# Where the operands of a matmul stand in SBUF: shifts of 32, 64 and 256 bytes

## The reference

```python
def _swiglu(x, w_gate, w_up, w_down):
    return (jax.nn.silu(x @ w_gate) * (x @ w_up)) @ w_down
...
h = _layer_norm(ALPHA * h + 0.5 * _swiglu(h, ffn1...), ln1_g, ln1_b)
mix = _token_mixers(h, w_in, ...)                  # 1024 -> 3072, recurrence and gating, -> 1024
h = _layer_norm(ALPHA * h + mix, ln2_g, ln2_b)
xa = _memory_cross_attention(h, mem, ...)          # q, k, v and output, 1024 x 1024 each
h = _layer_norm(ALPHA * h + xa, ln3_g, ln3_b)
h = _layer_norm(ALPHA * h + 0.5 * _swiglu(h, ffn2...), ln4_g, ln4_b)
...                                                # second block
h = rmsnorm(x, norm1_g)
x = x + concatenate([attention_mixer(...), pool_mixer(...)]) @ w_out
h = rmsnorm(x, norm2_g)
x = x + (silu(h @ w_gate) * (h @ w_up)) @ w_down
```

## Time and profile before

| | |
|---|---|
| median of the two runs | 1665.95 us |
| profiled execution, span | 1663.7 us |
| TensorE busy, matmuls | 1653.9 us (99%), 8375 |
| weight loads, beside the matmuls | 1393.3 us (84%) |
| GpSimd, VectorE, ScalarE busy | 704.5, 629.7, 597.6 us |
| mean granted TensorE clock | 0.999 of full |
| transfers | 157.58 MB, mean 95 GB/s |

### The profile page before, as it was taken

One profiled execution on the slowest core, in us unless ns is written; L12 is line 12 of the kernel. 1 busy time (PEld: TensorE's weight loads), 2 busy tenths in 40 slices (PEclk: granted clock), 3 DMA queues, 4 the chain that ended last, 5 costly groups with the idle time before them and its releaser, 6 DMA issues.

```text
span 1663.7 us, 20763 instructions
## 1 busy us (share of the span) xinstructions
PE 1653.9 (99%) x8375; PEld 1393.3 (84%) x8375; DVE 629.7 (38%) x1059; ACT 597.6 (36%) x911; POOL 704.5 (42%) x392
## 2 busy tenths in 40 slices
PE   9999999999999999999999999999999999999999
PEld 7888888899888888889888888898768988888888
DVE  4111121257565777656121111257763512121122
ACT  4122222247545555436221222247574322122220
POOL 4454444554572443133454444444323444344442
PEclk9999999999999999999999999999999999999999
DMA  7333243333222444123333243351113333323332
GB/s 208 91 102 92 83 117 89 101 104 111 77 64 64 127 129 144 57 77 89 91 99 101 74 117 99 92 156 42 44 32 80 86 101 93 97 83 110 99 89 77
DMA packets 296041, 157.58 MB, mean 95 GB/s; under 512 B 5265, under 2 KB 292618, under 8 KB 295946
## 3 DMA queue, kind: packets, MB, share of 16 engines
q1 hardware_dynamic: 295946, 156.26, 32.8%
HBM read 154.14 MB, written 2.10 MB: 94 GB/s over the span
## 4 chain that ended last, share of the span: by engine, by line
PE 93%; DVE 3%; ACT 2%; issue 1%; DMA 1%; POOL 0%; SPq 0%; DVEq 0%; POOLq 0%
PE bank L551 22%; PE bank L552 22%; PE bank L555 22%; PE bank L2349 2%; PE bank L2353 2%; PE bank L2350 2%; PE bank L594 2%; PE bank L595 2%; PE bank L599 2%; PE bank L2846 2%; PE bank L574 1%; PE bank L580 1%; PE bank L575 1%; PE bank L2834 1%; PE bank L2375 1%; PE bank L2594 1%
## 5 line engine op out<-in xcount | busy, mean ns | idle before, releaser
L479 POOL TENSOR_TENSOR wlo<-wraw,whi 128x1024 fp32r<-128x1024 f32 (+1 forms) x238 | 561.4, 2372 | 771.3 <-ACT whi L474 771.3
L551 PE MATMUL bank<-ahi,whi 128*128 128x512 f32 x1294 | 507.8, 392 | 0.0
L552 PE MATMUL bank<-alo,whi 128*128 128x512 f32 x1294 | 503.8, 389 | 0.0
L474 ACT CAST whi<-wraw 128x1024 fp32r<-128x1024 f32 (+1 forms) x268 | 268.0, 1025 | 232.6 <-PE bank L555 152.9
L555 PE MATMUL bank<-ahi,wlo 128*128 128x512 f32 x1294 | 320.9, 389 | 0.0
L551 PEld LDWEIGHTS bank<-ahi,whi 128*128 128x128 f32 x1294 | 243.0, 188 | 51.4 <-issue 1.2
L552 PEld LDWEIGHTS bank<-alo,whi 128*128 128x128 f32 x1294 | 242.9, 188 | 51.2 <-issue 1.4
L555 PEld LDWEIGHTS bank<-ahi,wlo 128*128 128x128 f32 x1294 | 242.9, 188 | 50.4
L1649 DVE SCALAR_TENSOR_TENSOR hval<-gate,bank 128x512 f32<-128x512 f32 x66 | 45.4, 687 | 554.4 <-PE bank L555 540.2
L1044 ACT ACTIVATE gate<-bank 128x512 f32<-128x512 f32 x66 | 39.5, 598 | 512.8 <-PE bank L555 500.6
L1658 DVE SCALAR_TENSOR_TENSOR res<-res,bank 128x512 f32<-128x512 f32 x78 | 52.7, 685 | 236.3 <-PE bank L555 163.8
(11 more groups left out here) (380 smaller groups left out, 2285.0 us busy)
## 6 DMA issues: line engine op xcount, KB each, us to landing
wraw<-in_ffn_w_gate SPq DMA_DIRECT2D x42, 512.0 KB, 3.9
wraw<-in_ffn_w_up SPq DMA_DIRECT2D x42, 512.0 KB, 3.9
wraw<-in_ffn_w_down SPq DMA_DIRECT2D x32, 512.0 KB, 3.6
wraw<-in_w_in SPq DMA_DIRECT2D x30, 512.0 KB, 4.0
wraw<-in_w_gate SPq DMA_DIRECT2D x21, 512.0 KB, 3.9
wraw<-in_w_up SPq DMA_DIRECT2D x21, 512.0 KB, 3.9
wraw<-in_w_out SPq DMA_DIRECT2D x16, 512.0 KB, 5.2
wraw<-in_w_down SPq DMA_DIRECT2D x16, 512.0 KB, 3.7
```

The costliest lines, as they stand in the source:

```text
L474: eng.copy(high_of(b)[:, 0:n], raw_of(b)[:, 0:n]).then_inc(hi_ready, 1)
L479: eng.tensor_tensor(low_of(b)[:, 0:n], raw_of(b)[:, 0:n], high_of(b)[:, 0:n], ALU.subtract).then_inc(LO[b][0], 1)
L551: eng.matmul(o, w, xhi[:, k, :], start=(k == 0), stop=False)
L552: eng.matmul(o, w, xlo[:, k, :], start=False, stop=False)
```

## The change

Two things change. First, the places of three tiles. `ahi` starts 32 bytes further, `alo` 64 bytes further than they would without a gap, and the tiles behind them move up by 512, so that their remainders stay; `hid` starts 256 bytes lower. The remainders modulo 512 are then: `ahi` 160, `alo` 192, `wraw`, `wlo`, `whi` 128 as before, `hid` 384, the early tiles 192 as before. Second, `multiply_tokens` finds its slots by the places in the rings and not by the block's own number. For the high weights that is the same slot (284 and 268 are both 0 modulo 4). For the low weights it is another: 284 modulo 6 is 2, 276 modulo 6 is 0, and the two blocks' low parts lie in slots 0 and 1.

The instructions and their order are the same on every engine.

```diff
@@ -111,8 +111,10 @@
         res = sb("res", [P, KD, T])
-        ahi = sb("ahi", [P, KD, T], F32R)
-        alo = sb("alo", [P, KD, T], F32R)
+        base = top[0]
+        ahi = sb("ahi", [P, KD, T], F32R, at=base + 32)
+        alo = sb("alo", [P, KD, T], F32R, at=base + 64 + KD * T * 4)
+        top[0] = base + 2 * KD * T * 4 + ROW
         wbase = top[0]
         wraw = sb("wraw", [P, RAW, SLOT])
@@ -151,7 +153,7 @@
         WORK = 16 * KB
-        take = region(WORK)
+        take = region(WORK - ROW // 2)
         hid = take("hid", [P, max(PARTS), 2, T], F32R)
@@ -2488,7 +2490,7 @@
             def multiply_tokens(ph):
                 b = ph.base + LAST
-                at = b % 4, b % RAW
+                at = HI_AT[b] % 4, RAW_AT[b] % RAW
                 wait_hi(pe, b + 1)
```

## The result

The changed kernel takes 1684.09 us at the median (1683.87 to 1684.31) against 1665.95 before: ratio 1.0113, 95% interval 1.0094 to 1.0132. It is 18.1 us slower, clear of noise and under 2%. The forecast was 1667, so the time is inside the range, but by the branch in which full blocks lose their settled pace (which I gave 0.13 for a loss under 2%), and not by the one I took. That the range holds it is owed to its width and not to the mechanism I chose.

What follows compares the result with a forecast made beforehand. The prediction took TensorE's matmul pace, busy 99% of the span, as the bound. Span 1663.7 plus 1.2 us (halved blocks; all other terms 0) gave 1664.9, plus 2.25 from span to median 1667.1, forecast 1667, range 1622 to 1699.

Steps and rivals of the forecast that it cites:

- the full blocks lose the settled pace: Rival: 512-column matmuls off distance 0 slow by 4.5 ns (+24.5 us) or to 232 ns (+29 us); chance 0.22, 0.13 under 2%.
- What bounds it: Whole kernel: TensorE busy 99% of 1663.7 us, almost no idle time to win, so only its matmul pace is left.
- Step 1: Full blocks, 5448 matmuls of 512 columns: pace stays 226.7 ns, change 0; bounds -66 to +29 us.
- the rival of a gain: Distance frees the full blocks: 17, 36 or 66 us less (1650, 1630, 1600); chances 0.10, 0.13, 0.11, together 0.34.
- My upper bound of 5.3 ns a matmul: Full blocks: up by the worst pace seen at this width, 232 ns; +5.3 x 5448 = +29 us.
- Step 2: Halved blocks, 1536 matmuls: +1.2 us from 384 with `alo` at distance 0, rest 0; bounds -5.7 to +4.6 us.
- Step 3: Last two blocks: low parts read from slots 0 and 1, 0; `hid` 256 away, at most -0.6 us, taken as 0.
- Step 4: ScalarE, VectorE, GpSimd at new offsets: idle time covers it; even twice TensorE's waits for them would be some 4 us.

## Why the prediction was right and wrong

**What bounds it** was right: TensorE's pace is all there is, and the whole change of the span is found in it, with no wait longer by more than 0.1 us.

**Step 1, full blocks, failed for `ahi` and `alo`.** I took 0 because 544 cycles for 512 columns is the same 17/16 as 272 for 256, and read that as a limit of the stream which placing could not touch. Down, that is what 12 distances show: none is faster, so the rival of a gain, which I had given 0.34, did not come at any of them. Up, it is wrong: 544 is what two of twelve distances give, the others 549 to 562. The term, put at 0, measured 19.4 us: 18.7 in `multiply` and 0.7 in the other full blocks on `ahi` and `alo`. My upper bound of 5.3 ns a matmul, the pace right behind a restart, held for the changed kernel (5.0) but not as a bound: 32 bytes for both parts cost 6.6 ns (5.60 us a block), and -96 bytes 7.6 (5.62). For `hid`, 1344 matmuls at distance 256, step 1 was right within a nanosecond.

The rival "the full blocks lose the settled pace" is what happened, on the 4104 matmuls on `ahi` and `alo` and not on 5448, which is why the loss stayed under its 24.5 us. It had two sizes, 4.5 ns from the halved blocks and 5.3 from the pace behind a restart; the 5.0 measured lies between them. The argument that halved blocks speed up at a distance of 64 was no argument for full blocks: with the weights 64 above, which is -64, full blocks take 5.60 us.

In this operand type and at this width the trace of before held a number for the loss and none for the gain: 232 ns behind a restart, and after it 226.7 always. I still gave the loss 0.22 and the gain 0.34. The trace knew only distance 0 at this width, so the chances should have leaned to the side for which it had a row. That blocks off distance 0 are slow for the same reason as those behind a restart is not shown; only their paces are alike.

**Step 2, halved blocks,** gave +1.2 us from `alo` at distance 0. Measured: the durations in the group L2350 went from 279 to 281 ns and in L2375 from 279 to 281, 2 ns and not 3. From start to start, which is the pace, the 384 matmuls with `alo` took only 0.4 us more. Those with `ahi`, put at 0, took 0.4 too, and those with `hid` nothing: 0.8 in all. The 120.0 for distance 0 is confirmed where both operands stand there, in the kernel with both 64 up:

```profile
744.14 1.12 PE L2355 MATMUL bank<-ahi,wlo 128*128 128x256 f32 x8
747.02 1.12 PE L2355 MATMUL bank<-ahi,wlo 128*128 128x256 f32 x8
```

2.88 / 24 = 120.0. `hid` at 320 from the weights runs as at 64, both paces, as a period of 256 says (changed kernel, first half, second half):

```profile
359.61 1.11 PE L2355 MATMUL bank<-hid,wlo 128*128 128x256 f32 x8
362.44 1.11 PE L2355 MATMUL bank<-hid,wlo 128*128 128x256 f32 x8
...
371.73 1.07 PE L2355 MATMUL bank<-hid,wlo 128*128 128x256 f32 x8
374.45 1.07 PE L2355 MATMUL bank<-hid,wlo 128*128 128x256 f32 x8
```

**Step 3, the last two blocks:** 0, as forecast. They still take 120.0 ns with `hid` 256 away (16 matmuls from 1670.26 to 1672.18 us). **Step 4:** no wait of TensorE grew by more than 0.1 us; all together are 5.8 us against 6.8 before. **Not in the sum at all** were the memory keys, which gave back 2.0 us (last point of this text); without them the two spans would differ by some 20 us.

**The Trainium skill** (TensorE: Matmul & The Clock Gate, step 1 of Part 2) says that loading the next weights takes no read bandwidth from the running matmul. If so, where the weights stand could not slow the matmul beside which they load, and here it does: with the operands left in place, moving the high weights by 32 bytes cost 24.9 us (1690.21 against 1665.36), the loads themselves staying at 188 ns. The measurement decides. The runs show only that the pair matters, not where in the chip the two meet.

**What stays open:** why 0 and 256 are the good distances; why the operand pays 12 ns above half of a plain float32 pass (428 ns) even there; what chooses between the two paces of the halved blocks; why `alo` alone at 64 slows the matmuls at distance 0 too; and what sets the pace of the memory keys.

## What to carry to other kernels

When TensorE never waits, read its pace from start times a whole block apart and compare it over stretches; a few ns on thousands of equal matmuls can be the largest term there is (here 4.7 ns on 4104 matmuls, 19 us). Keep the moving operand and the weights that load beside it at the same byte remainder (here modulo 256), in float32r with 512 columns, and measure each distance on the chip before trusting a rule for it. The pace of the unsettled stretches of the old trace was a fair guess for a layout that the trace had never seen, but no bound: 232 ns there, up to 234 with the worst distance.

## What the runs showed of the hardware that was not expected

- The pace of a 512-column float32r matmul depends on the distance between the moving operand and the weights being loaded beside it: 226.7 ns at 0 and -256 bytes, 229 at 64, up to 234 at -96, at a granted clock of 0.999 to 1.0 throughout. The loads stay at 188 ns, in the changed kernel as before.
- It is the weights being loaded, not those being multiplied: with only the high weights moved, the last low-weight matmul of a block takes 234.9 ns, those before it 227.
- A distance of -16 bytes costs as much as 32 or -32 (5.60 us a block for each).
- The sign counts: 64 above the weights 5.49 us, 64 below 5.60.
- Matmuls at distance 0 ran at 231 ns in place of 226.7 behind a stretch that alternates between 0 and 64; behind a stretch wholly at -32 they were back at 227 after one. Only one kernel shows the first.
- The memory keys, whose tiles kept their distance to their weights, changed pace all the same: one of their groups went from 289 ns to 285, and their 192 matmuls of 256 columns from 24.5 us to 22.5, start to start. The moved distances do not do it: with everything 32 bytes up, every distance as before, they take 22.5 too. Before and in the changed kernel:

```profile
L551 PE MATMUL bank<-mhi,whi 128*128 128x256 f32 x48 | 12.0, 289 | 0.0
...
L553 PE MATMUL bank<-mhi,whi 128*128 128x256 f32 x48 | 11.6, 285 | 0.0
```
